# Layer norms whose scale and shift are folded into a later eviction, with the residual completed on GpSimd

## The reference, cut to what matters

```python
h = x * (1 + scale1) + shift1
y = token_mixer(h, ...)                      # attention beside spatial gating
x = layer_norm(ALPHA * x + gate1 * y, ln1_g[l], ln1_b[l])
h = x * (1 + scale2) + shift2
y = moe_ffn(h, ...)                          # router, 64 experts, top 8, one shared expert
x = layer_norm(ALPHA * x + gate2 * y, ln2_g[l], ln2_b[l])
```

## Time and profile before

| | us |
|---|---|
| median of 3 runs | 2992.61 (2990.23 to 2993.92) |
| the profiled execution | 2994.28 |
| its span | 2992.5 |
| busy in the span | PE 2798.5, PEld 2077.7, DVE 1629.0, ACT 756.6, POOL 409.8 |
| mean granted TensorE clock | 0.984 of full speed |

### The profile page before, as it was taken

How to read it: one execution, slowest core, us unless ns; L and a number is a source line. 1 busy time by engine, 2 the same in 40 slices (tenths; PEclk the granted TensorE clock), 3 DMA queues, 4 the chain that set the end, 5 groups by cost and what they waited for, 6 DMA issues and landing times.

```text
span 2992.5 us, 65346 instructions
## 1 busy us (share of the span) xinstructions
PE 2798.5 (94%) x27418; PEld 2077.7 (69%) x27418; DVE 1629.0 (54%) x2821; ACT 756.6 (25%) x1400; POOL 409.8 (14%) x343
## 2 busy tenths in 40 slices
PE   7999999988899999999989899999998999899998
PEld 6878566655587866655557588844577887888973
DVE  6745433333473554444436478788757536555555
ACT  0122212121112133323213422200045414443210
POOL 1000000000000000000000036400014302434630
PEclk9999999999999999999999999999999999999999
DMA  9945999999984599999974035485430023000443
GB/s 392 389 161 219 406 405 415 386 421 420 389 365 141 205 381 420 419 407 420 420 310 141 15 113 171 168 308 197 154 106 18 4 82 129 18 16 33 157 167 112
DMA packets 102704, 718.31 MB, mean 240 GB/s; under 512 B 11680, under 2 KB 11968, under 8 KB 18176
## 3 DMA queue, kind: packets, MB, share of 16 engines
q1 hardware_dynamic: 98448, 700.02, 59.5%
q0 software_dynamic: 3952, 14.00, 1.5%
HBM read 711.09 MB, written 2.88 MB: 239 GB/s over the span
## 4 chain that ended last, share of the span: by engine, by line
PE 74%; DVE 12%; DMA 9%; ACT 2%; issue 2%; SPq 0%; POOL 0%; DVEq 0%; ACTq 0%; POOLq 0%
PE ps L229 16%; PE ps L1614 10%; PE ps L2167 9%; PE ps L2192 7%; DMA arena<-in_w_up 6%; DVE arena L162 6%; PE ps L3139 5%; PE ps L1643 5%; PE ps L2832 3%; PE ps L1705 2%; ACT arena L145 2%; DMA arena<-in_w_down 2%; DVE arena L166 2%; PE ps L2559 1%; PE ps L3571 1%
## 5 line engine op out<-in xcount | busy, mean ns | idle before, releaser
L145 ACT ACTIVATE arena<-ps 128x512 f32<-128x512 f32 (+3 forms) x529 | 266.9, 505 | 1268.0 <-PE ps L229 244.7
L229 PE MATMUL ps<-arena 128*128 128x256 f32 x2144 | 480.1, 385 | 18.5 <-DMA arena<-in_w_in 4.9
L162 POOL TENSOR_TENSOR arena<-arena 128x512 f32<-128x512 f32 (+1 forms) x288 | 376.4, 1307 | 821.7 <-DVE arena L162 284.4
L229 PEld LDWEIGHTS ps<-arena 128*128 128x128 f32 x2144 | 408.7, 192 | 87.1 <-issue 9.7
L1614 PE MATMUL ps<-arena 128*32 128x256 f32 (+2 forms) x5120 | 390.8, 389 | 42.0 <-DMA arena<-in_w_up 31.0
L1614 PEld LDWEIGHTS ps<-arena 128*32 128x32 f32 (+2 forms) x5120 | 248.5, 120 | 187.4 <-issue 87.8
L162 DVE TENSOR_TENSOR arena<-ps,arena 128x256 f32<-128x256 f32 (+3 forms) x416 | 203.8, 490 | 235.0 <-PE ps L3139 87.9
L162 DVE TENSOR_TENSOR arena<-arena 128x512 f32<-128x512 f32 (+6 forms) x473 | 294.1, 622 | 60.7 <-PE ps L2192 35.7
L2167 PE MATMUL ps<-arena 128*128 128x256 f32 (+1 forms) x1792 | 298.5, 328 | 2.2 <-DVE arena L162 1.5
L2192 PE MATMUL ps<-arena 128*128 128x512 f32 x672 | 293.0, 593 | 2.4 <-DVE arena L162 2.2
L2167 PEld LDWEIGHTS ps<-arena 128*128 128x128 f32 x1792 | 270.0, 191 | 29.6 <-DVE arena L171 3.3
(11 more groups left out here) (278 smaller groups left out, 2912.1 us busy)
## 6 DMA issues: line engine op xcount, KB each, us to landing
arena<-in_w_gate SPq DMA_DIRECT2D x128, 1024.0 KB, 13.0
arena<-in_w_up SPq DMA_DIRECT2D x128, 1024.0 KB, 14.1
arena<-in_w_down SPq DMA_DIRECT2D x128, 1024.0 KB, 13.5
arena<-in_mlp SPq DMA_DIRECT2D x80, 1024.0 KB, 4.8
arena<-in_w_ada SPq DMA_DIRECT2D x48, 1024.0 KB, 13.1
arena<-in_ada SPq DMA_DIRECT2D x48, 1024.0 KB, 4.9
arena<-in_w_in SPq DMA_DIRECT2D x30, 1024.0 KB, 11.3
arena<-in_w_rkv SPq DMA_DIRECT2D x20, 1024.0 KB, 4.9
```

The lines of the kernel that those rows point to most:

```text
L145: self.e.activation(out, in_, func, bias=bias, scale=scale, **more).then_inc(*self.done(key))
L162: self.e.tensor_tensor(out, a, b, op).then_inc(*self.done(key))
L229: ins = pe.matmul(out, a, b, start=start and i == 0, stop=stop and i == len(pairs) - 1)
```

## The change

The norms now write only (x - mean)/std to XS: `ln_factors` makes 1/std and -mean/std, and one pass of 128x512 per half row is made on each of VectorE and ScalarE (`normed_half`). The turned tokens get g and b by the eviction that was there: `folded` puts b * (1 + scale) into shift and g into (1 + scale), three operations on 128x8. After the transposes, GpSimd makes XS whole for the residual (`whole_pool`: XS times g, plus b, two operations of 128x1024 per token half); in an expert stage it waits for XH and XL of that half, and it runs in experts 0, mixer 1 and experts 1. At the start of attention, g and b of the last norm are applied where the turned tokens are evicted.

In the last of the 26 rounds the sums get YF itself in full precision, in 4 calls, in place of YH and YL in 8, and the rounding and the subtraction of that round are left out. The statistics are taken bank by bank.

So that g and b outlive their stage, the mixer's memory is laid out anew; hT, PP, PT and qT now lie where the expert stage's last slots and the context's rows were, and in mixer 1 ScalarE and VectorE wait for the event `c kept` before they write there. The tables of the second norm are no longer loaded in experts 1.

```diff
-        def ln_rest(dve, do, key, t, g, bvec, dst, i):
-
-            f = slice(i * 1024, i * 1024 + 1024)
-            do.stt(t[:, f], t[:, f], LN[1][:, i, 0:1], g, ALU.subtract, ALU.mult)
+        def ln_factors(dve, do, key, i):
+
+            rstd, shift = (LN[n][:, i:i + 1] for n in (2, 3))
             dve.wait_ge(*at["ln root", key, i])
-            do.rcp(LN[2][:, i:i + 1], LN[2][:, i:i + 1])
-            do.stt(dst[:, f], t[:, f], LN[2][:, i:i + 1], bvec, ALU.mult, ALU.add, ("ln", key, i))
+            do.rcp(rstd, rstd)
+            do.ts(shift, LN[1][:, i, 0:1], rstd, -1.0, ALU.mult, ALU.mult, ("ln factors", key, i))
...
+        def normed_half(do, key, src, i, h, done=None):
+
+            dst = XS[:, i * 1024 + h * 512:i * 1024 + h * 512 + 512]
+            do.fma(dst, src, LN[2][:, i:i + 1], LN[3][:, i:i + 1], ("ln", key, i, h))
...
+        def folded(do, l, which, g, b):
...
+            do.tt(both_, vec(b), scale, ALU.mult)
+            do.tt(shift, shift, both_, ALU.add)
+            do.tt(scale, scale, vec(g), ALU.mult)
...
+        def whole_pool(pool, l, which, t, g, b):
+
+            do, f = VectorSteps(pool, filled), slice(t * 1024, t * 1024 + 1024)
+            do.tt(XS[:, f], XS[:, f], g, ALU.mult)
+            do.tt(XS[:, f], XS[:, f], b, ALU.add, ("whole", l, which, t))
...
+            if l:
+                pool.wait_ge(*at["moe", l - 1])
+                pool.wait_ge(*at["turned", l, 0, 3])
+                for t in range(2):
+                    whole_pool(pool, l, 0, t, E.lg, E.lb)
...
+            pool.wait_ge(*at["turned", l, 1, 3])
+            for t in range(2):
+                pool.wait_ge(*at["high", l, t])
+                pool.wait_ge(*at["low", l, t])
+                whole_pool(pool, l, 1, t, M.lg, M.lb)
...
+                def last_add(nh):
+                    reach(pe, *at["yf", l, p, nh])
+                    for t in range(2):
+                        pe.matmul(psum.tiles[ACC + t * 2 + nh][:, :], f32(E.ST[p % 2][:, t * 128:t * 128 + 128]),
+                                  E.YF[:, nh * 512:nh * 512 + 512], start=False, stop=True).then_inc(*made(("last added", l, nh, t)))
...
+        def turned_tokens(eng, do, k2):
+
+            eng.wait_ge(*at["columns", 0, k2])
+            for k in (2 * k2, 2 * k2 + 1):
+                do.fma(B.xv[:, k, :], psum.of["columns", 0, k2][:, k % 2 * 256:k % 2 * 256 + 256], vec("ln2g1")[:, k:k + 1],
+                       vec("ln2b1")[:, k:k + 1], ("columns out", 0, k2) if k % 2 else None)
```

More of the change, by code:

```diff
@@ L573, in turned_pe @@
                     keep_warm(pe, spare, 2 if which else 5)
-                reach(pe, *at[ready(t)])
+                for key in ready(t):
+                    reach(pe, *at[key])
                 for k2 in range(4):
@@ L934, in mixer_pe @@
                     keep_warm(pe, b, 4)
-            turned_pe(pe, l, 0, lambda t: ("ln", ("moe", l - 1), t) if l else "x")
+            turned_pe(pe, l, 0, lambda t: [("ln", ("moe", l - 1), t, h) for h in range(2)] if l else ["x"])
             if l == 0:
@@ L1130, in mixer_dve @@
                 do.tt(M.yv[:, mt, :], M.yv[:, mt, :], M.GSv[:, 8 + mt, :], ALU.add, ("y done", l) if mt == 7 else None)
-            dve.wait_ge(*at["mixer", l])
+            folded(do, l, 1, f"ln1g{l}", f"ln1b{l}")
+            if l:
+                dve.wait_ge(*at["whole", l, 0, 1])
+            else:
+                folded(do, 1, 0, "ln2g0", "ln2b0")
             for t in range(2):
@@ L1497, in moe_pe @@
         def moe_pe(pe, l):
-            turned_pe(pe, l, 1, lambda t: ("ln", ("mixer", l), t))
+            turned_pe(pe, l, 1, lambda t: [("ln", ("mixer", l), t, h) for h in range(2)])
             turned_done(pe, l, 1)
@@ L1716, in moe_pe @@
                 if p >= 0:
-                    add(1)
+                    (add if new is not None else last_add)(1)
                 psum.among = (p % 2,)
@@ L1753, in moe_act @@
                 if p >= 0:
-                    for nh in range(2):
+                    for nh in range(2 if p < NR - 1 else 0):
                         act.wait_ge(*at["yf", l, p, nh])
@@ L1779, in moe_act @@
                 early_act(act, do, l, p, 2)
-            ln_act(act, do, ("moe", l))
+            for t in range(2):
+                ln_root(act, do, ("moe", l), t)
+            for t in range(2):
+                act.wait_ge(*at["ln factors", ("moe", l), t])
+                normed_half(do, ("moe", l), psum.tiles[ACC + t * 2 + 1][:, :], t, 1, ("sum out", l, t * 2 + 1))
             end(("moe", l), "act", acted)
@@ L1904, in moe_dve @@
                 early_dve(dve, do, l, p, 0)
+                if p == 0:
+                    dve.wait_ge(*at["whole", l, 1, 1])
                 if p >= 0:
@@ L1911, in moe_dve @@
                                ALU.mult, ALU.mult, ("yf", l, p, nh))
-                    for nh in range(2):
+                    for nh in range(2 if new is not None else 0):
                         y = slice(nh * 512, nh * 512 + 512)
@@ L1958, in moe_dve @@
             for t in range(2):
-                for nh in range(2):
-                    f = slice(nh * 512, nh * 512 + 512)
-                    do.stt(E.hT[:, t * 1024 + nh * 512:t * 1024 + nh * 512 + 512], psum.tiles[ACC + t * 2 + nh][:, :],
-                           LN[1][:, t, 0:1], E.lg[:, f], ALU.subtract, ALU.mult, ("sum out", l, t * 2 + nh))
-                dve.wait_ge(*at["ln root", ("moe", l), t])
-                do.rcp(LN[2][:, t:t + 1], LN[2][:, t:t + 1])
-                f = slice(t * 1024, t * 1024 + 1024)
-                do.stt(XS[:, f], E.hT[:, f], LN[2][:, t:t + 1], E.lb, ALU.mult, ALU.add, ("ln", ("moe", l), t))
+                ln_factors(dve, do, ("moe", l), t)
+                normed_half(do, ("moe", l), psum.tiles[ACC + t * 2][:, :], t, 0, ("sum out", l, t * 2))
             end(("moe", l), "dve", formed)
@@ L2537, in attention_pe @@
                 projected(mt, 1, "context")
-            reach(pe, *at["ln", ("moe", 1), 1])
+            for h in range(2):
+                reach(pe, *at["ln", ("moe", 1), 1, h])
             turning_pe(pe, 0, XS[:, :])
@@ L2604, in attention_act @@
             for k2 in (1, 3):
[L2605 to L2606 removed]
+                turned_tokens(act, do, k2)
             for k2 in range(4):
@@ L4100, in layout @@
         put(f"b_sp{l}", np.ascontiguousarray(I["b_spatial"][l].T))
+    for l in range(2):
+        put(f"ln1g{l}", vi(I["ln1_g"][l]))
+        put(f"ln1b{l}", vi(I["ln1_b"][l]))
+        put(f"ln2g{l}", (vs if l else vi)(I["ln2_g"][l]))
+        put(f"ln2b{l}", (vs if l else vi)(I["ln2_b"][l]))
     b2 = I["ada_b_2"]
```

68 lines of the change are left out of this document (39 added, 29 removed).

## The result

| kernel | median us | executions | ratio to the kernel before, 95% interval |
|---|---|---|---|
| before | 2991.42 | 4 (2989.79 to 2993.92) | |
| after | 3012.07 | 4 (3005.35 to 3017.05) | 1.0066 (1.0049 to 1.0083) |
| after, once more | 3011.22 | 6 (3009.06 to 3014.83) | 1.0056 (1.0039 to 1.0073) |

The change makes the kernel slower: by 20.7 us in the first comparison, by 16.8 in the second, where 23 executions of the kernel before had a median of 2994.38. The forecast was 3007.4, 14.8 above the 2992.61 that the kernel before had then, range 2997 to 3018; both medians lie just above 3004 to 3011, the likeliest case's own range. The profiled execution of after took 3005.35 us (span 3003.6), the fastest of its four.

A forecast was written before the change was run, and what follows sets the result against it. VectorE's routing chain was taken to set the pace before the weight stream, fillers binding elsewhere. Blocking 14.2 + clock 1.4 - 0.4 (experts to mixer) - 0.4 (into attention) = +14.8 us on 2992.61: 3007.4, range 2997 to 3018.

The forecast's parts named there:

- the likeliest case: Whole kernel: the forecast itself, 3007.4 us, with its own range of 3004 to 3011; chance 0.55.
- GpSimd beside VectorE: Routing in each expert stage: four GpSimd operations block VectorE instructions with SBUF inputs, 7.9 us lost per stage.
- The 0.37: Routing: the time before GpSimd's end at which VectorE is released, by the long row; the small row gave 0.16.
- The clock: Gather in the expert stages: TensorE stands longer and runs partly at 1.2 GHz; 1.4 us added for the first stage.
- Mixer to experts: Mixer to experts boundary, twice: shorter norm lets router matmuls start at 264.8 instead of 265.6, fillers limiting; 0.8 us gained each.
- Experts to mixer: End of experts to second mixer: norm 5.6 us shorter, but TensorE's fillers set the time; 0.4 us gained.
- Into attention: Start of attention: first context projection's bank free 1.4 us sooner, scaled evictions 1.0 us longer; 0.4 us gained.
- Second mixer: Second mixer: GpSimd's four operations cost VectorE's modulation sums 8.4 us, taken up by 8.7 of waiting; 0 taken.
- Rival 1: Routing, both expert stages: VectorE's short operations slip through, only the 2.4 us of gains remain, 2990.2 us; chance 0.07.
- rival 2: Routing, both expert stages: half the blocking, 7 us instead of 15, 3000 us; chance 0.15.
- rival 4: Second mixer leaks: VectorE's loss delays weight slots and the rotation; up to 8.4 us more, 3015.8 us; chance 0.2.
- rival 5: Expert stage: waits make GpSimd finish after 304 us and round 0 stops for it; chance 0.03.

The follow-up runs named there:

- afterwarm: The changed kernel with fillers in TensorE's two idle times per expert stage (12 calls instead of 3, 9 new ahead of the gather): 3008.6 us, ratio 1.0049.
- latewarm: late with 7 filler calls instead of 3 ahead of the routing's first counts, boundary fillers unaltered: 2989.68 us, ratio 0.9993.
- beforewarm: The kernel before with 7 filler calls instead of 3 ahead of the routing's first counts, nothing else: 2993.56 us, ratio 1.0007.
- beforelast: The kernel before with only the last round's addition in full precision: 2993.92 us, ratio 0.9997.
- nowhole: The changed kernel with GpSimd's two 1024-column instructions per half replaced by one of a single column, in all three places: 2992.92 us, ratio 0.9990.
- late: The changed kernel with GpSimd's four instructions put behind VectorE's last routing instruction, beside the gather: 2992.64 us, ratio 0.9991.
- latefew: late with fewer TensorE fillers at the boundaries (9 calls instead of 14; none between halves instead of 5 or 2): 2994.63 us, ratio 0.9999.
- again: The changed kernel once more, unaltered, against the kernel before: 3011.22 us, ratio 1.0056.
- beforepool: The kernel before with four 128x1024 GpSimd additions per expert stage where the changed kernel has its own, nothing else of the change: 3010.81 us, ratio 1.0055.

## Why the prediction was right

**GpSimd beside VectorE, 7.9 us in each expert stage: right.** The rows give 7.92. With the clock taken out, afterwarm against latewarm is 31.6 less 23.8 and 31.6 less 23.7: 7.8 and 7.9 us. The places were the four predicted (copy and sum behind the first half, the two seat comparisons behind the second), and so was the wait of an instruction, about 2.1 and not the whole 2.35. Two small errors cancel in the sum: the first half lost 4.2 where 3.95 was worked out, because the 0.25 hidden behind the wait for the scores fell to an instruction that ran ahead of GpSimd, and the second lost 3.8 where 4.0 was. The release was read well from the short row and not from the long one: GpSimd's first instruction runs from 269.91 for 2.48, to 272.39, and the copy that ends at 272.55 needs 0.29 of its own, so it began 0.13 before GpSimd's end (the 0.16 of the prediction). The 0.37 took for granted that the long sum was issued as GpSimd's instruction began, and that this one kept its 1.27.

**The clock, 1.4 us in the first stage: mis-sized.** I took over the 5.45 us gather of the earlier trace rows for both stages. It takes 6.36 and 6.39, and the small counts ahead of it slow down too. By afterwarm the low clock costs 2.37 and 2.32; the kernel before already paid 1.35 (25.78 less beforewarm's 24.43). So by these profiles the term is 3.3 us and not 1.4: behind two waits of 4 us the clock cost more than behind the one wait of 1.7 from which I had my row. How much the kernel before pays differs from stage to stage, though: over the ten stages with that idle time the cost was nothing in two, 0.2 in one, 1.3 to 1.5 in six and 2.6 in one (beforelast), 1.1 in the mean. With twice that mean for the kernel before, the term would be 2.4.

**Mixer to experts, 0.8 gained each time: near, 1.1.** From the output projection's start (228.73 before, 229.87 after) to the end of the transposes it is 33.9 against 33.5, and from there to the gate beforewarm has 24.5 and latewarm 23.8: 0.4 + 0.7 = 1.1. The fillers did bind, as said: the router's matmuls (265.84) start where they end.

**Experts to mixer, 0.4 gained: 0.3.** XS was whole 5 us ahead of the second transposes, as forecast, and nothing came of it until the fillers were cut.

**Into attention, 0.4 gained: wrong in sign, 0.3 lost.** TensorE's rows in after, and the first of them in the kernel before, last:

```profile
1555.32 14.05 PE L229 MATMUL ps<-arena 128*128 128x256 f32 x64 [1.29 <-DVE XS L171]
...
1569.21 1.91 PE L2569 MATMUL ps<-ident,XS 128*128 128x128 f32 x16
1574.77 8.70 PE L229 MATMUL ps<-arena 128*128 128x256 f32 x32 [3.66 <-DVE gates L166]
...
1538.73 14.05 PE L229 MATMUL ps<-arena 128*128 128x256 f32 x64 [1.81 <-DVE arena L166]
```

The wait in front of the next projections is 3.66 us and not the 2.66 of the earlier trace rows: the scaled evictions cost 1.0 more, as forecast. The step that failed is the bank of the first context projection, which was to come free 1.4 us sooner. Counted from the last down product (1548.06 and 1530.79), that projection starts at 7.3 us where the kernel before has 7.9: 0.7 sooner, so the next ones start 0.3 later. beforelast says where the rest went. With the full precision round alone the same projection starts at 6.3. The new norm gives 0.9 of these 1.6 us back: the kernel before's first pass over the bank needs only the mean and follows the statistics at once (1537.83 behind 1537.80), while the one pass of the change needs 1/std first and starts at 1554.36, 0.9 us behind its statistics (1553.45).

**Second mixer, 0 of up to 8.4: right.** VectorE does lose there: its 28 sums between the first projection and the rotation take 41.8 us, not 36.0. Its idle time takes that up. The sums over columns begin at 862.03 in after, 39.7 us behind the mixer's first projection (822.33); in the kernel before it is 852.16 behind 812.46, the same. The loss was 5.8 us, and not 8.4, for only three of the long sums met the four GpSimd instructions. Leaving the four out (nowhole) changes no time.

Sum of the terms as measured: 2 x 7.9 + 3.3 - 2 x 1.1 - 0.3 + 0.3 = 16.9 us, where 14.8 was forecast; the second comparison has 16.8. That they agree so closely is in part luck, as the clock's term shows. The first comparison's 20.7 comes with four executions a side, and no profile shows its other 4. The two profiled executions differ by only 11.1 us in span: behind the last down product of the second expert stage the one of after happened to take 6.2 less (1455.5 against 1461.7), a part that takes from 1455.5 to 1468.9 in the profiles at hand.

One thing the sum doesn't say: without GpSimd's price, by the profiles, the change gains 2 x 1.1 + 0.3 - 0.3 = 2.2 us, and the full precision round alone, in beforelast, 0.3 + 1.6 = 1.9. The difference, 0.3, is what is left for the fold itself, which no run has alone: what it gains at the two mixer to experts boundaries it gives back going into attention. All of these are too small for the medians to show. Rival 1 (no blocking) and rival 2 (half) fall to the rows of 2.35, 2.79 and 4.64; rival 4 to nowhole; rival 5 to the first round's scaling, which waits for nothing of GpSimd's. That every VectorE instruction with SBUF inputs stands was too wide: a TENSOR_REDUCE doesn't, as the same section of the Trainium skill says; here the four blocked ones were all of the kinds that do.

## What to carry to other kernels

Work given to GpSimd because it has time isn't free for VectorE: here a VectorE instruction with two SBUF inputs, or a copy of 256 columns within SBUF, stood nearly as long as the GpSimd instruction that it met, however short it was itself. So put such work beside VectorE's PSUM reads or waits (one semaphore gave back 18.6 us), or cut it into pieces (13.7). Before shortening a norm, see whether TensorE waits for the norm or for its own filler: by the profiles, cutting fillers at one boundary, where the change had the tokens ready 5 us early, gave 4.3 us, and all parts of the change without GpSimd 2.2. And when a change has several parts, run each alone: by the profiles the part that gained most here was not the one that the change is named for.

## What the hardware showed that I had not expected

- TensorE's clock fell after an idle time of only 1.7 us, between short runs of matmuls: in the expert stages with that idle time a stretch at the lower level followed at the gather in 7 of 10 (profiles of before, late, nowhole, latefew, beforelast), in those whose idle time was filled in none of 10. Its length was 3.4 us by the clock records in six and 6.8 in one, beforelast's, which cost 2.6 us. With the two waits of 4 us it lasted 13.7, in all four stages of after and again, and cost 2.3 and 2.4 in after.
- GpSimd's 128x1024 multiplication or addition takes 2.35 to 2.5 us from two sources (late, after) and 1.9 where both are the same (beforepool).
- In pieces, GpSimd and VectorE alternate, one instruction each: GpSimd's piece of 256 columns takes 0.73 to 0.85 us beside VectorE instructions of 128 and 256 columns, and 1.06 beside the one of 512.
- Beside VectorE sums of 1024 columns GpSimd's own instructions stretch too: 11.70 us for four in the second mixer, 9.73 in the expert stage.
